# A depthwise convolution spread over three engines, and two of its eight chunks moved to ScalarE and GpSimd

## The reference

```python
CONV_WIDTH = 31
def conformer_conv(h, w_pw1, b_pw1, w_dw, b_dw, ln_g, ln_b, w_pw2, b_pw2):
    a, gt = jnp.split(h @ w_pw1 + b_pw1, 2, axis=-1)
    z = a * jax.nn.sigmoid(gt)
    z = lax.conv_general_dilated(
        z, w_dw[:, None, :], window_strides=(1,), padding=[(CONV_WIDTH - 1, 0)],
        dimension_numbers=('NWC', 'WIO', 'NWC'), feature_group_count=D_MODEL) + b_dw
    z = jax.nn.silu(layernorm(z, ln_g, ln_b))
    return z @ w_pw2 + b_pw2
```

## Time and profile before

| what | value |
|---|---|
| median of 3 runs | 2897.31 us (2896.39 to 2903.05) |
| the profiled execution | 2897.87 us, span 2895.7 us |
| TensorE busy | 2772.3 us, 96% |
| VectorE, ScalarE, GpSimd busy | 1968.0, 1158.2, 100.5 us |
| granted TensorE clock | 0.98 of full speed over the span |
| first products of the convolution layer | 1866.3 to 2047.1 us of the span |
| taps and folds on TensorE, three chunks | 2047.1 to 2105.5 us |
| the mean is there | 2110.9 us |

### The profile page before, as it was taken

How to read it: one execution, slowest core, us unless ns; L and a number is a source line. 1 busy time by engine, 2 the same in 40 slices (tenths; PEclk the granted TensorE clock), 3 DMA queues, 4 the chain that set the end, 5 groups by cost and what they waited for, 6 DMA issues and landing times.

```text
span 2895.7 us, 39549 instructions
## 1 busy us (share of the span) xinstructions
PE 2772.3 (96%) x15525; PEld 2260.7 (78%) x15525; DVE 1968.0 (68%) x3222; ACT 1158.2 (40%) x2049; POOL 100.5 (3%) x109
## 2 busy tenths in 40 slices
PE   6999999899999999999999999899979999999999
PEld 4878875677878876788888888688667888888887
DVE  6435225686356664687787778689965887777885
ACT  4333226533147784333333344411153423333443
POOL 1030020000400000000000000000000000000000
PEclk9999999999999998999999999899989999999999
DMA  7030210142100003233322563211003332335632
GB/s 285 17 86 23 66 44 10 45 116 88 33 8 2 1 2 110 91 113 117 117 102 100 213 208 91 62 57 39 17 30 102 117 107 98 108 111 198 226 95 102
DMA packets 187040, 257.31 MB, mean 89 GB/s; under 512 B 29766, under 2 KB 138730, under 8 KB 182250
## 3 DMA queue, kind: packets, MB, share of 16 engines
q1 hardware_dynamic: 182672, 232.45, 24.6%
q10 hardware_dynamic: 4185, 22.35, 1.9%
HBM read 186.62 MB, written 67.11 MB: 88 GB/s over the span
## 4 chain that ended last, share of the span: by engine, by line
PE 69%; DVE 7%; ACT 1%; issue 1%; DMA 0%; ACTq 0%; DVEq 0%
PE ps L1658 28%; PE ps L1666 14%; PE ps L1611 11%; PE ps L1434 4%; PE ps L1537 2%; PE ps L1488 2%; PE ps L1506 2%; PE ps L1722 2%; PE ps L1151 1%; PE ps L1773 1%; PE ps L1030 1%; PE ps L1759 0%; PE ps L1412 0%; PE ps L1547 0%; PE ps L1482 0%
## 5 line engine op out<-in xcount | busy, mean ns | idle before, releaser
L1658 PE MATMUL ps<-x_ops,w_ring 128*128 128x512 f32 x3696 | 840.3, 389 | 7.0 <-ACT even_rows L2290 3.9
L1658 PEld LDWEIGHTS ps<-x_ops,w_ring 128*128 128x128 f32 x3696 | 693.3, 188 | 152.1 <-issue 8.6
L1666 PE MATMUL ps<-a_ring,w_ring 128*128 128x512 f32 x1848 | 419.5, 389 | 0.0
L1666 PEld LDWEIGHTS ps<-a_ring,w_ring 128*128 128x128 f32 x1848 | 346.8, 188 | 72.4 <-DVE w_ring L3044 0.5
L1611 PE MATMUL ps<-h_high,ring_parts 128*128 128x512 f32 x1024 | 320.2, 394 | 17.9 <-DVE h_low L2512 9.2
L2232 ACT ACTIVATE w_ring<-ring 128x512 fp32r<-128x512 f32 x230 | 144.2, 629 | 301.3 <-PE ps L1658 284.7
L1611 PEld LDWEIGHTS ps<-h_high,ring_parts 128*128 128x128 f32 x1024 | 193.5, 190 | 63.0 <-issue 12.9
L2475 DVE TENSOR_TENSOR ring_parts<-ring,ring_parts 128x1024 fp32r<-128x1024 f32 (+2 forms) x77 | 93.9, 1221 | 199.9 <-ACT ring_parts L1858 199.4
L1611 PE MATMUL ps<-h_low,ring_parts 128*128 128x512 f32 x512 | 200.8, 392 | 0.0
L3044 DVE TENSOR_TENSOR w_ring<-ring,w_ring 128x512 fp32r<-128x512 f32 x230 | 158.0, 687 | 38.7 <-ACT w_ring L2232 38.7
L1858 ACT ACTIVATE ring_parts<-ring 128x1024 fp32r<-128x1024 f32 (+2 forms) x77 | 75.9, 990 | 255.5 <-PE ps L1611 177.0
(11 more groups left out here) (497 smaller groups left out, 4554.2 us busy)
## 6 DMA issues: line engine op xcount, KB each, us to landing
a_raw<-act_kept SPq DMA_DIRECT2D x70, 512.0 KB, 3.8
act_kept<-even_rows SPq DMA_DIRECT2D x12, 1536.0 KB, 5.1
act_kept<-odd_rows SPq DMA_DIRECT2D x10, 1536.0 KB, 5.1
ring<-in_ffn_w_gate_dram SPq DMA_DIRECT2D x12, 1024.0 KB, 5.8
ring<-in_ffn_w_up_dram SPq DMA_DIRECT2D x12, 1024.0 KB, 6.1
ring<-in_conv_w_pw_dram SPq DMA_DIRECT2D x24, 512.0 KB, 3.9
late<-in_ffn_w_gate_dram SPq DMA_DIRECT2D x10, 1024.0 KB, 5.7
late<-in_ffn_w_up_dram SPq DMA_DIRECT2D x10, 1024.0 KB, 6.0
```

The costliest lines, as they stand in the source:

```text
L1658: last = mm(o, w_ring[:, i % 4, wp_, P * k:P * k + P], x_ops[:, X_OP[p], rp_, k, :], start=p in "176" and k == 0 and p_ == 0, stop=k == 3 ...
L1666: last = mm(bank(OUT_BANK[DOWN_GROUP[p] + c_]), w_ring[:, (A_UNITS + b) % 4, wp_, P * c_:P * c_ + P], a_ring[:, b % 4, rp_, :], start=p in ...
```

## The change

The chunks are divided anew. VectorE convolves chunks 0, 2, 4 and 5 (four, not five), TensorE chunks 6 and 7 (two, not three), and chunks 1 and 3 are done by ScalarE and GpSimd together: GpSimd makes the two difference planes (128x526 and 128x527), ScalarE makes the product of a plane with a tap (an activation with a scale by partition, 128x512), and GpSimd adds it to the accumulator (128x512), 46 times a chunk. Three product buffers go round, so product i waits for addition i-3. ScalarE's 47 products of a chunk are put into its program by portions: six after the sigmoids of chunks 2 to 7, six after the high parts that follow the up products of chunks 1 to 7, six more behind the last of them, and twice five between the copies of TensorE's first chunk. GpSimd starts on chunk 1 when it is gated. VectorE's sum for the mean now waits for `pool_chain` before it adds chunk 1, and again before chunk 3. TensorE's waits for `zc_ok_pe` count two chunks. The tap tiles are two instead of three, and the accumulators and product buffers lie in memory that is free at that time.

```diff
--- before.py
+++ after.py
@@ -243,8 +243,12 @@
         zp = part(8192, (KC, 2, HALF))
         zc = zp[:, :, :, 0:S // 2]
         flat_sc = sc[:, :, :].rearrange("p a b -> p (a b)")
-        tap_tiles = flat_sc[:, 0:3 * CONV_W * 32].rearrange("p (c t n) -> p c t n", c=3, t=CONV_W)
-        stacked = flat_sc[:, 3 * CONV_W * 32:3 * CONV_W * 32 + 32]
+        tap_tiles = flat_sc[:, 0:2 * CONV_W * 32].rearrange("p (c t n) -> p c t n", c=2, t=CONV_W)
+        stacked = flat_sc[:, 2 * CONV_W * 32:2 * CONV_W * 32 + 32]
+        pool_rest = flat_sc[:, 2016:2016 + HALF - 1]
+        far = place("far", [P, 4, 512], A_DISTS + 4 * 512)
+        pool_acc, pool_other = far[:, 0, :], far[:, 1, :]
+        tap_products = [far[:, 2, :], far[:, 3, :], flat_sc[:, 2544:3056]]
         quarter_sums = [part(17648 + 512 * i, (512,)) for i in range(7)] + [dists[:, 0:512]]
         sg = part(16624, (S,))
         later = part(21616, (HALF - 1,))
@@ -602,7 +606,8 @@
 
         N_PAR = 21
         N_PW = 0
-        PE_CONV = (KC - 3, KC - 2, KC - 1)
+        POOL_CONV, PE_CONV = (1, 3), (KC - 2, KC - 1)
+        POOL_BEFORE_CONV, POOL_STEPS = 87, 48
         H_MUL = {0: 0, 4: 8, 5: 16}
         H_HI = {0: 0, 2: 8, 4: 16, 5: 24}
         H_OK = {0: 0, 2: 8, 4: 16, 5: 24}
@@ -769,6 +774,8 @@
             return n == N_FIRST - 1 or first_units[n + 1].block != first_units[n].block
 
         x_kept = nc.dram_tensor("x_kept", [P, KC, S], F32)[:, :, :]
+
+        act_before_conv = [0]
 
         block = ctx.enter_context(nc.Block())
 
@@ -1743,10 +1750,10 @@
                 tap_sums(c_, 0)
                 fold(c_, 1)
                 fold(c_, 0)
-            pe.wait_ge(s.zc_ok_pe, 4)
+            pe.wait_ge(s.zc_ok_pe, 2)
             for half in range(2):
                 mm(bank(2 + half), ones[:, :], zc[:, KC - 2, half, :], start=True, stop=False)
-            pe.wait_ge(s.zc_ok_pe, 6)
+            pe.wait_ge(s.zc_ok_pe, 4)
             for half in range(2):
                 mm(bank(2 + half), ones[:, :], zc[:, KC - 1, half, :], start=False, stop=False)
             pe.wait_ge(s.zc_sum, KC - 3)
@@ -2371,15 +2378,60 @@
                 norm_high(4, k)
                 if k == 0:
                     high(T_PW1 + 1)
+            tap_at = [0]
+            act_before_conv[0] = chained[0]
+
+            def tap_product(q, i):
+
+                n = POOL_CONV[q]
+                even, odd = zp[:, n, 0, :], zp[:, n, 1, :]
+                done = POOL_BEFORE_CONV + POOL_STEPS * q + 2
+                chained[0] += 1
+                if i == 0:
+                    a.wait_ge(s.up_free, N_PW + n + 2)
+                    if q:
+                        a.wait_ge(s.pool_chain, POOL_BEFORE_CONV + POOL_STEPS * q)
+                    f(pool_acc, odd[:, 0:512], ACT.Identity, bias=cols[:, V_BDW + n:V_BDW + n + 1],
+                      scale=sum_taps[:, 0, n:n + 1]).then_inc(s.act_chain, 1)
+                    return
+                if i > 3:
+                    a.wait_ge(s.pool_chain, done + i - 3)
+                elif q:
+                    a.wait_ge(s.pool_chain, POOL_BEFORE_CONV + POOL_STEPS * (q - 1) + 2 + 46 - 3 + i)
+                if i < N_EVEN:
+                    src, k = odd[:, i:i + 512], None
+                elif i < N_EVEN + N_ODD:
+                    m = i - N_EVEN
+                    src, k = pool_rest[:, m:m + 512], 2 * m + 1
+                else:
+                    e = (i - N_EVEN - N_ODD + 1) % N_EVEN
+                    src, k = even[:, e:e + 512], 2 * e
+                if i == N_EVEN:
+                    a.wait_ge(s.pool_chain, done)
+                f(tap_products[(46 * q + i - 1) % 3], src, ACT.Copy,
+                  scale=sum_taps[:, i, n:n + 1] if k is None else cols[:, V_WDW + 8 * k + n:V_WDW + 8 * k + n + 1])\
+                    .then_inc(s.act_chain, 1)
+
+            def tap_product_steps(count):
+
+                for _ in range(count):
+                    tap_product(tap_at[0] // 47, tap_at[0] % 47)
+                    tap_at[0] += 1
+
             for n in range(KC):
                 a.wait_ge(s.gate_out, N_PW + n + 1)
                 if n < KC - 1:
                     high(T_PW1 + 2 * n + 2)
                 a.wait_ge(s.up_free, N_PW + n + 1)
                 f(sg, bank(0, 2), ACT.Sigmoid, bias=cols[:, V_BPW1 + 8 + n:V_BPW1 + 9 + n]).then_inc(s.gate_free, 1)
+                if n > 1:
+                    tap_product_steps(6)
                 if n < KC - 1:
                     a.wait_ge(s.up_out, N_PW + n + 1)
                     high(T_PW1 + 2 * n + 3)
+                if n >= 1:
+                    tap_product_steps(6)
+            tap_product_steps(6)
             for c_, n in enumerate(PE_CONV):
                 for turn, parity in enumerate((1, 0)):
                     a.wait_ge(s.conv_out, 2 * c_ + turn + 1)
@@ -2388,6 +2440,8 @@
                     for i in range(4):
                         last = f(quarter_sums[4 * parity + i], bank(4 * parity + i), ACT.Copy)
                     last.then_inc(s.conv_taken, 1)
+                    if c_ == 0:
+                        tap_product_steps(5)
                 for turn, parity in enumerate((1, 0)):
                     a.wait_ge(s.fold_out, 2 * c_ + turn + 1)
                     f(zc[:, n, parity, :], bank(4 * parity), ACT.Identity,
@@ -3449,19 +3503,19 @@
             low(T_PW1 + 2)
             between(0); convolve(0, range(0, 8)); low(T_PW1 + 4); convolve(0, range(8, 18))
             between(1); convolve(0, range(18, 25)); low(T_PW1 + 6); convolve(0, range(25, STEPS))
-            between(2); convolve(1, range(0, 9)); low(T_PW1 + 8); convolve(1, range(9, 18))
-            between(3); convolve(1, range(18, 24)); low(T_PW1 + 10); convolve(1, range(24, STEPS))
-            between(4); convolve(2, range(0, 8)); low(T_PW1 + 12); convolve(2, range(8, 17))
-            between(5); convolve(2, range(17, 24)); low(T_PW1 + 14); convolve(2, range(24, STEPS))
-            between(6); convolve(3, range(0, 18))
-            between(7); convolve(3, range(18, STEPS))
-            convolve(4, range(0, STEPS))
+            between(2); convolve(2, range(0, 9)); low(T_PW1 + 8); convolve(2, range(9, 18))
+            between(3); convolve(2, range(18, 24)); low(T_PW1 + 10); convolve(2, range(24, STEPS))
+            between(4); convolve(4, range(0, 8)); low(T_PW1 + 12); convolve(4, range(8, 17))
+            between(5); convolve(4, range(17, 24)); low(T_PW1 + 14); convolve(4, range(24, STEPS))
+            between(6); convolve(5, range(0, 18))
+            between(7); convolve(5, range(18, STEPS))
             planes = lambda row: row.rearrange("p (two m) -> p two m", two=2)
-            v.wait_ge(s.zc_ok, KC - 3)
+            v.wait_ge(s.zc_ok, KC - 4)
+            v.wait_ge(s.pool_chain, POOL_BEFORE_CONV + POOL_STEPS)
             tt(planes(sc[:, 3, :]), zc[:, 0], zc[:, 1], add).then_inc(s.zc_sum, 1)
             for k in range(2, KC - 2):
-                if k in PE_CONV:
-                    v.wait_ge(s.zc_ok_pe, 2)
+                if k == POOL_CONV[1]:
+                    v.wait_ge(s.pool_chain, POOL_BEFORE_CONV + 2 * POOL_STEPS)
                 v.wait_ge(s.zc_sum, k - 1)
                 tt(planes(sc[:, 3, :]), planes(sc[:, 3, :]), zc[:, k], add).then_inc(s.zc_sum, 1)
             v.wait_ge(s.mean_done, 1)
@@ -3604,6 +3658,23 @@
             stage(g, "mixer_attended")
             stage(g, "x_3")
             g.memset(zp[:, :, :, 0:HALF - 512], 0.0).then_inc(s.pad_ok, 1)
+            assert chained[0] == POOL_BEFORE_CONV
+            for q, n in enumerate(POOL_CONV):
+                even, odd = zp[:, n, 0, :], zp[:, n, 1, :]
+                g.wait_ge(s.up_free, N_PW + n + 2)
+                chain(g.tensor_tensor(pool_rest, even[:, 1:], odd[:, 0:HALF - 1], ALU.subtract))
+                chain(g.tensor_tensor(even, even, odd, ALU.subtract))
+                for i in range(1, 47):
+                    g.wait_ge(s.act_chain, act_before_conv[0] + 47 * q + i + 1)
+                    if i < N_EVEN:
+                        o, old = pool_acc, pool_acc
+                    elif i < N_EVEN + N_ODD:
+                        o = zc[:, n, 1, :] if i == N_EVEN + N_ODD - 1 else pool_other
+                        old = pool_acc if i == N_EVEN else pool_other
+                    else:
+                        o = zc[:, n, 0, :] if i == 46 else pool_acc
+                        old = pool_acc
+                    chain(g.tensor_tensor(o, old, tap_products[(46 * q + i - 1) % 3], ALU.add))
 
 
 # ---- launch: one core; inputs and outputs as the reference has them
```

## The result

The changed kernel takes 2971.51 us (median of 4 runs, 2969.12 to 2972.41) against 2899.23 (4 runs): 1.0248 times as long, 95% interval 1.0235 to 1.0261. The forecast was 2962.4 us, slower.

The account below looks back on a forecast made before the run. TensorE was taken to set the pace, VectorE ending its share within 3 us of it. Held turns, less the removed chunk, put the mean 65.1 us later: 2962.4 us on the median's base, range 2930 to 2995.

Parts of the forecast that it names:

- GpSimd and VectorE take turns: On SBUF, GpSimd additions and VectorE instructions reading two SBUF tensors never overlap; times add, convolution steps included; PSUM reads escape.
- The price of a turn: VectorE's held time per 512-column GpSimd addition: 1.07 us, with ends 0.85 and 1.32.
- the sum: From chunk 6's gating through chunk 7's and TensorE's two chunks to the mean: 65.1 us later, at 2176.0.
- 6 hidden: Us taken off the held time: 5 under gatings up to chunk 6's, one more before chunk 7's.
- its 68: Turns before chunk 6's gating: 2 subtractions and 6 + 5 x 12 additions, at 1.07 us 72.8.
- Who waits for whom: In the first products, VectorE's gating period grows from 22 to some 35 us; TensorE waits at the gate; ScalarE needs 25.
- Rival 1: GpSimd gets only every third turn, two VectorE steps passing per addition: 2978 us, chance 0.15.
- The tail: From chunk 7's gating at 2135.4 through TensorE's taps, copies, ScalarE's last products and second chunk to the mean at 2176.0.
- ScalarE's last five products: Before TensorE's first chunk is written: three at 0.63 us, two waiting for additions at 1.8 each, some 4.8 in all.
- 65.1: Us by which the mean was forecast to come later than at 2110.92, all of the forecast loss.
- VectorE just behind TensorE: At the stage's end, VectorE's share ends at 2172, just before TensorE's 2176; it sets nothing by 4 us.
- Rival 3: VectorE's multiply-and-add is not held at all, TensorE's path decides: 10.9 us faster, 2887 us, chance 0.07.

Follow-up runs that it names:

- no_read: The changed kernel with GpSimd's 92 additions replaced by memsets that read no SBUF, all waits kept, sums of chunks 1 and 3 not made: 2887.3 us.
- one_read: The changed kernel with GpSimd's 92 additions replaced by a multiplication with one that reads one SBUF tensor, sums not made: 2912.7 us.
- half_cols: The changed kernel with GpSimd's 92 additions over 256 columns instead of 512, half of each sum not made: 2918.6 us.
- in_psum: The changed kernel with VectorE's accumulators in PSUM for chunks 0, 2, 4 and the first part of 5, everything computed: 2894.5 us.
- gaps: The changed kernel with each VectorE step of chunk 5's second part waiting for the one just before, not the last but one: 2964.6 us.
- in_psum_7: Like in_psum, with ScalarE's products in portions of seven instead of six, three after the last up product, none between TensorE's copies: 2884.5 us.

## Why the prediction was right, point by point

- **GpSimd and VectorE take turns.** Shown, by no_read, one_read, half_cols and in_psum together, for the multiply-and-add too. The Trainium skill (SBUF — State Buffer, section Who interferes with whom) adds that a GpSimd instruction that only writes does not contend with a VectorE instruction of two SBUF inputs; no_read agrees, 0.78 us beside 84 us of memsets.
- **The price of a turn, 1.07 us.** A little high. From the second gating to the seventh chunk's 82.3 us were added (212.4 - 130.1), where the sum has 72.8 + 19.3 less 6 hidden, 86.1. The sum counts 86 turns in it, the trace 90 GpSimd instructions (the 68 and 22 of the first two stretches). That its 68 are met is luck: they are 64 additions and the four subtractions of both chunks, where the sum has 66 and two. And 22, not 18, fall before chunk 7's gating, since five of the ten products between TensorE's copies are made before it. So a turn cost 0.91 us, hiding included, where the sum has 1.00. In the bursts a step and an addition together take 1.69; alone, steps follow each other by 0.79 where each waits for the last and by 0.66 where they overlap, so a turn is 0.90 or 1.03.
- **Who waits for whom.** The period is as forecast, 34.9 us from gating to gating in the mean (174.7 in five; forecast some 35), TensorE waits with the fall of its granted clock that was to be covered, and ScalarE is no pacemaker. The sum lets TensorE wait for the gatings; in the trace what came last in its ten waits in the first products, 44.5 us, is VectorE's low part of the weights, which stands in VectorE's program behind a gating or among the held steps. Only the taps' second half waits for a gating (15.3). Rival 1 (every third turn) is not what the bursts show: one to one.
- **The tail** was sized too low: 40.6 us from gating 7 to the mean, measured 50.5. Two terms. TensorE's clock: after its waits the half chunk took 10.63 instead of 8.2 (granted 0.79) and the second chunk 18.96 instead of 16.3 (granted 0.86), 5.1 us together, which the sum had covered in the first part and forgot here, where nothing covers it. And ScalarE's last five products: from the copies' end to the chunk's writing 9.4 instead of 4.8, by the one held addition; gaps gives these 4.6 back. The two errors, -3.8 up to gating 7 and +9.9 behind it, are the 6.1 between 65.1 and 71.2; that they partly cancel is luck.
- **VectorE just behind TensorE.** Its sum ended at 2162.17 + 3.74 = 2165.9 and then it waited 19.5 us for TensorE, not 4: TensorE's tail was longer, and VectorE's last steps ran in part alone (six turns were left, not ten).
- **Rival 3 (no hold, 2887)** is near what the kernel would take without the exclusion: no_read, with all its waits, takes 2887.3. That the two numbers agree so well is in part luck: GpSimd's pace was 1.41 us in the rival's sum, and a memset takes 0.96.

## What to carry to other kernels

GpSimd is no free third engine beside a VectorE that streams two SBUF operands: price each GpSimd instruction that reads SBUF as its read time on VectorE, and look in the trace for a longer VectorE instruction just where GpSimd began one. Where the work must lie there, put one of VectorE's operands into PSUM: here that turned +2.5% into -0.2% (in_psum), and -0.5% with ScalarE's portions changed as well (in_psum_7). And after a move has made an engine wait, price its clock in the part where nothing covers it.

## What the runs showed that was not expected

- Exclusion is not always one to one. While VectorE's steps overlap (one begins 0.08 us before the other ends), an addition of the changed kernel once waited 6.31 us for a row of them, and in one_read two copies of 0.62 us took over 7.8; in half_cols one addition of 256 columns took 8.51. The 6.31 ended at the first step that waited for its predecessor, 2153.62, which was held itself. VectorE in order of time, then GpSimd:

```profile
2152.18 0.74 DVE L3488 SCALAR_TENSOR_TENSOR big<-big,cols,sc 128x512 f32<-128x512 f32 x1
2152.84 0.74 DVE L3490 SCALAR_TENSOR_TENSOR sc<-big,cols,sc 128x512 f32<-128x512 f32 x1
2153.62 1.63 DVE L3490 SCALAR_TENSOR_TENSOR big<-big,cols,sc 128x512 f32<-128x512 f32 x1
...
2148.39 7.98 POOL L3677 TENSOR_TENSOR far<-far 128x512 f32<-128x512 f32 x2 [11.26 <-ACT far L2411]
```

  The run gaps takes the overlap away, and with it the long addition. In other bursts the same kind of steps let GpSimd in at each turn; what decides between the two is open.
- VectorE's product of a plane with scalars (L3478, one SBUF operand, 0.548 us in the kernel before) was held too: 0.55 us before GpSimd began, some 1.39 in the other three.

```profile
L3478 DVE TENSOR_SCALAR sc<-big,cols 128x512 f32<-128x512 f32 x4 | 4.7, 1182 | 0.1
```

  In no_read it took 1.00 us at 1992.02, beside a memset that began at 1991.79: this form was held by an instruction that only writes, where the steps, at 0.78, were not:

```profile
1992.02 1.00 DVE L3478 TENSOR_SCALAR sc<-big,cols 128x512 f32<-128x512 f32 x1
...
1991.79 0.95 POOL L3680 MEMSET far<- 128x1024 f32 x1
```

  The Trainium skill (SBUF — State Buffer, section Who interferes with whom) says that a tensor-scalar operation can enter a mode that uses two ports, and that VectorE in such a mode contends with GpSimd. The trace agrees in the hold; it does not show the mode.
